# Recurrence preparation spread over the token-shift tiles, filter weights as sums and differences, expert slabs read among the last dense slabs

## Time and profile before

| | |
|---|---|
| median of three runs | 2147.86 us |
| the profiled execution | 2153.43 us |
| its span | 2151.6 us |
| mean granted TensorE clock | 0.923 |
| PE busy | 1889.2 us (88%) |
| DVE busy | 624.7 us (29%) |
| ACT busy | 295.8 us (14%) |
| POOL busy | 79.5 us (4%) |
| HBM read | 423.02 MB |
| expert slabs | 189 whole, 6 halves |

### The profile page before, as it was taken

The page is one execution under the profiler, slowest core; times in us unless marked ns, Lnnn a source line. Parts: engine busy times, 40 slices in busy tenths (PEclk is TensorE's granted clock), DMA queues, the critical chain, the costliest instruction groups (busy, mean ns, idle before and its releaser), DMA issues.

```text
span 2151.6 us, 26763 instructions
## 1 busy us (share of the span) xinstructions
PE 1889.2 (88%) x10986; PEld 1306.1 (61%) x10986; DVE 624.7 (29%) x1253; ACT 295.8 (14%) x664; POOL 79.5 (4%) x95
## 2 busy tenths in 40 slices
PE   7999999999999999999999997999997656565665
PEld 2444445888874787679889985887777212121212
DVE  4544445031432213624000348250434000000001
ACT  2200000011210012402000233211322000000001
POOL 1000000010000000001000102120001000000000
PEclk9999999999999999989999999797998788786868
DMA  8544444444432122136446731000238899999995
GB/s 325 181 165 170 173 175 163 145 151 157 149 126 71 51 95 98 59 134 220 153 156 240 250 137 59 3 3 20 79 118 329 361 421 421 422 422 422 422 422 242
DMA packets 64248, 425.45 MB, mean 198 GB/s; under 512 B 7283, under 2 KB 7764, under 8 KB 16988
## 3 DMA queue, kind: packets, MB, share of 16 engines
q1 hardware_dynamic: 54576, 387.05, 46.9%
q10 hardware_dynamic: 9580, 37.05, 4.9%
HBM read 423.02 MB, written 1.05 MB: 197 GB/s over the span
## 4 chain that ended last, share of the span: by engine, by line
PE 30%; DMA 19%; DVE 3%; SPq 1%; issue 1%; POOL 1%; ACT 1%; POOLq 0%; ACTq 0%; DVEq 0%
PE bank L785 19%; DMA arena<-experts_dram 19%; PE bank L1220 3%; PE bank L1470 2%; PE bank L1099 1%; SPq L708 1%; PE bank L1289 1%; DVE arena L2391 1%; PE bank L1306 1%; PE bank L1304 1%; PE bank L1292 0%; PE bank L1345 0%; PE bank L1392 0%; PE bank L1320 0%; POOL rstd L735 0%
## 5 line engine op out<-in xcount | busy, mean ns | idle before, releaser
L785 PE MATMUL bank<-arena 128*128 128x256 f32 (+2 forms) x4864 | 1117.6, 391 | 4.6 <-DVE arena L2266 2.0
L785 PEld LDWEIGHTS bank<-arena 128*128 128x128 f32 x4864 | 832.6, 192 | 280.0 <-issue 199.8
L1470 PE MATMUL bank<-arena 128*32 128x512 f32 x1536 | 251.4, 816 | 182.5 <-DMA arena<-experts_dram 182.5
L1470 PEld LDWEIGHTS bank<-arena 128*32 128x32 f32 x1536 | 66.5, 143 | 361.6 <-issue 361.6
L2091 DVE TENSOR_TENSOR arena<-sil,bank 128x512 f32 (+3 forms) x44 | 24.4, 554 | 275.9 <-PE bank L785 265.8
L2582 DVE TENSOR_TENSOR arena<-arena,bank 128x512 f32<-128x512 f32 x8 | 5.5, 689 | 275.4 <-PE bank L1470 275.4
L1604 ACT ACTIVATE sil<-bank 128x512 f32<-128x512 f32 (+1 forms) x44 | 21.6, 491 | 401.8 <-PE bank L785 239.8
L1220 PE MATMUL bank<-arena 64*64 64x64 f32 x2048 | 66.4, 227 | 7.8 <-POOL arena L754 5.5
L1220 PEld LDWEIGHTS bank<-arena 64*64 64x64 f32 x2048 | 65.4, 143 | 9.3 <-POOL arena L754 5.7
L2097 DVE SCALAR_TENSOR_TENSOR sq<-arena 128x1024 f32<-128x1024 f32 x56 | 68.4, 1222 | 1.5
L2098 DVE SCALAR_TENSOR_TENSOR arena<-arena 128x1024 f32<-128x1024 f32 x56 | 68.3, 1220 | 0.0
(11 more groups left out here) (331 smaller groups left out, 1418.3 us busy)
## 6 DMA issues: line engine op xcount, KB each, us to landing
arena<-experts_dram SPq DMA_DIRECT2D x189, 1024.0 KB, 22.9
arena<-dense_dram SPq DMA_DIRECT2D x167, 1024.0 KB, 4.8
arena<-ada_rest_dram ACTq DMA_DIRECT2D x56, 512.0 KB, 3.8
arena<-ada_head_dram SPq DMA_DIRECT2D x8, 1024.0 KB, 25.4
arena<-experts_dram SPq DMA_DIRECT2D x6, 512.0 KB, 22.8
arena<-tokens_dram ACTq DMA_DIRECT2D x1, 2048.0 KB, 22.5
arena<-masks_dram ACTq DMA_DIRECT2D x1, 1184.0 KB, 5.1
arena<-decay_dram ACTq DMA_DIRECT2D x1, 1024.0 KB, 15.8
```

The lines of the kernel that those rows point to most:

```text
L785: ins = mm(out, lhsT=w, rhs=rhs(k), start=k == 0, stop=k == k_tiles - 1)
L1470: ins = mm(ps[banks[half]][32 * e:32 * e + 32, :], lhsT=lhs[:, 2 * kp + par, CAP * e:CAP * e + CAP], rhs=slab[e][par][:, half * 512:half * ...
```

## The change

Four edits.

1. **Filter.** The third sine layer stands ahead of the first conditioning product. It is computed twice, on partitions 0 to 63 and 64 to 127 (`filt_w3` laid out twice), and of the second copy only column 0 is used, with its sign turned; the rest of those rows is zero. w4 comes as 128 rows, and POOL makes sum and difference of its halves once. Eight products by these give sum and difference at once, four of them over 128 rows; DVE has one multiplication for each. The second conditioning product is moved between the two halves.
2. **Preparation.** Its steps are placed between the shift tiles on each engine; `k_dir` goes to POOL; the low-rank products use banks 7, 5 and 6; ACT takes the gate's sigmoid after the aq tiles; `BT`, `KT` and `QQ` are made in the order in which they are wanted, with events of their own; AM is cleared in three parts.
3. **Expert slabs.** SP issues twelve ring slabs and one of the three extra ones between the dense slabs 151 to 163, then four and the two others. The extra three are now slabs 16 to 18.
4. **End.** The last four slabs come in halves, all first halves ahead of all second ones, and ACT loads the square root's table before the last group's copies.

```diff
             pe.wait_ge(filters_in, 32)
             sine_layer(0)
             sine_layer(1)
+            sine_layer(2)
             pe.wait_ge(cond_ready, 1)
             ada_sums("ada_head", 0, 0)
-            sine_layer(2)
...
+            pe.wait_ge(w4_ready, 2)
             pe.wait_ge(sin_ready, 3)
             for n in range(8):
+                half, tt, part = n // 4, n // 2 % 2, n % 2
+                rows = (P, 64)[tt]
+                take(pe, "w4", n % 4, half)
+                mm(ps[n % 4][:, :], lhsT=fh[0:rows, tt * P:tt * P + P], rhs=w4_parts[part][0:rows, half * 512:half * 512 + 512],
+                   start=True, stop=True).then_inc(full[n % 4], 1)
+                if n == 3:
+                    ada_sums("ada_head", 0, 1)
...
@@ gpsimd
+            pool.wait_ge(w4_in, 16)
+            for n, op in enumerate((add, sub)):
+                nc.gpsimd.tensor_tensor(w4_parts[n], w4[:, 0:D], w4[:, D:2 * D], op).then_inc(w4_ready, 1)
...
+            pool.wait_ge(mu_ready, 1)
+            for n in range(4, 8):
+                evacuated(pool, "lora", *lora_at(n))
+            for d in range(2):
+                for j in range(4):
+                    nc.gpsimd.tensor_scalar(kd256[:, 4 * d + j, :], iclr[:, 4 * d + j, :], c("ka", j), tiny[:, 28 + j:29 + j],
+                                            mult, add).then_inc(kd_scaled, 1)
+            pool.wait_ge(kkr_ready, 1)
+            for d in range(2):
+                pool.wait_ge(kd_scaled, 4 * d + 4)
+                nc.gpsimd.tensor_tensor(kd256[:, 4 * d:4 * d + 4, :], kd256[:, 4 * d:4 * d + 4, :], US[:, US_K:US_K + 4, :], mult)\
+                    .then_inc(kd_ready, 1)
+            pool.wait_ge(kt_ready, 1)
+            nc.gpsimd.memset(page(19, 2048), 0.0).then_inc(am_zero, 1)
+            pool.wait_ge(exc_used, 1)
+            nc.gpsimd.memset(page(21, 4096), 0.0).then_inc(am_zero, 1)
             pool.wait_ge(qq_ready, 1)
-            nc.gpsimd.memset(page(19, 8192), 0.0).then_inc(am_zero, 1)
+            nc.gpsimd.memset(page(20, 2048), 0.0).then_inc(am_zero, 1)
@@ tensor
             for t in range(len(EARLY), 15):
                 b, use = shift_at(t)
                 take(pe, "shift", b, use)
                 product(ps[b][:, 0:T], KD, lambda k: h[:, k, :], full[b])
+                if t == 7:
+                    pe.wait_ge(masks_in, 48)
+                    kk_norm()
+                elif 8 <= t < 12:
+                    if t == 8:
+                        pe.wait_ge(act_us, 1)
+                        evacuated(pe, "shift", 1, 0)
+                    for n in range(2 * t - 16, 2 * t - 14):
+                        lora_up(n)
@@ scalar
+            def decays(d):
+                act.wait_ge(logs_ready, d + 1)
+                ...
+                A(Eneg[:, o, :], inc[:, o, :], ACT.Exp, scale=DECAY_SCALE)
+                A(Eexc[:, o, :], (D2, D1)[d][:, o, :], ACT.Exp, scale=(-DECAY_SCALE, DECAY_SCALE)[d])
+                A(Einc[:, o, :], inc[:, o, :], ACT.Exp, scale=-DECAY_SCALE)
+                A(scl[:, 4 * d:4 * d + 4], scl[:, 4 * d:4 * d + 4], ACT.Exp, scale=-DECAY_SCALE).then_inc(exps_ready, 1)
             for t in range(15):
                 b, use = shift_at(t)
                 got(act, "shift", b, use)
                 A(US[:, t, :], ps[b][:, 0:T], ACT.Copy, scale=rt[:, 256 + t:257 + t]).then_inc(us_scaled, 1)
+                if t == 6:
+                    evacuated(act, "shift", 0, 0)
+                    A(US[:, 0, :], US[:, 0, :], ACT.Tanh).then_inc(act_us, 1)
+                    act.wait_ge(kkr_ready, 1)
+                    A(gsq_kk, kkr_flat, ACT.Square).then_inc(kksq_ready, 1)
+                elif t == 8:
+                    act.wait_ge(ss_ready, 1)
+                    A(nrm, nrm, ACT.Sqrt).then_inc(nrm_ready, 1)
+                if 8 <= t < 12:
+                    for n in range(2 * t - 16, 2 * t - 14):
+                        lora_out(n)
+                elif t >= 13:
+                    decays(t - 13)
@@ vector
+            for t in range(15):
+                shifted(t)
+                if t == 5:
+                    kk_scaled()
+                elif t == 7:
+                    kk_sums()
+                elif t == 9:
+                    dve.wait_ge(nrm_ready, 1)
+                    do(V.reciprocal(nrm, nrm))
+                elif t == 11:
+                    decay_sums(0)
+                elif t == 12:
+                    decay_logs(0)
+                elif t == 13:
+                    decay_sums(1)
+                elif t == 14:
+                    decay_logs(1)
@@ sync
+            mixer2 = N_DENSE - 31
+            for m in range(first_mixed * RING, N_DENSE):
                 sp.wait_ge(slab_started, m - RING + 2)
                 sp.dma_start(ring_flat[m % RING], dram["dense"][m]).then_inc(slab_loaded[m % RING], 16)
+                if m == mixer2 + 15:
+                    got(sp, "gn", 3, 0)
+                    expert(0, 1, 2)
+                elif m == mixer2 + 21:
+                    evacuated(sp, "batt", 7, 3)
+                    sp.wait_ge(yr_ready, 1)
+                    expert(3, 4, 5)
+                elif m == mixer2 + 22:
+                    expert(6, 7)
+                elif m == mixer2 + 23:
+                    expert(8)
+                    got(sp, "proja", 3, 1)
+                    expert(9)
+                elif m == mixer2 + 24:
+                    expert_late(0)
+                elif m == mixer2 + 26:
+                    evacuated(sp, "projr", 3, 1)
+                    expert(10)
+                elif m == mixer2 + 27:
+                    expert(11)
+            got(sp, "wout", 3, 3)
+            expert(12, 13, 14, 15)
+            expert_late(1)
+            for half in range(2):
+                got(sp, "htok", 5 + half, 1)
+            expert_late(2)
...
+            for par in range(2):
+                for e in range(GROUP):
+                    j = rest - GROUP + e
+                    sp.wait_ge(ex_started, rounds * EX_RING + (j + EX_LATE) // GROUP * GROUP + 2 * GROUP)
+                    sp.dma_start(ex_flat[j][:, par * D:par * D + D], dram["experts"][12 * N_EXP - GROUP + e][:, par * D:par * D + D])\
+                        .then_inc(ex_last_in[e] if par else ex_loaded[j], 16)
```

More of the change, by code:

```diff
@@ L1136, in _, with kk_norm, lora_up @@
             half_tiles("shift", 5, shift_norms)
+            def kk_norm():
+                pe.wait_ge(kksq_ready, 1)
+                for i in range(2):
+                    take(pe, "kkn", 5 + i, 0)
+                    mm(ps[5 + i][:, :], lhsT=blk, rhs=gsq_kk[:, i * 512:i * 512 + 512], start=True, stop=True)\
+                        .then_inc(full[5 + i], 1)
+            def lora_up(n):
+                which, d, half = n // 4, n // 2 % 2, n % 2
+                b, use = lora_at(n)
+                take(pe, "lora", b, use)
+                for q_ in range(2):
+                    j = 2 * half + q_
+                    ins = mm(ps[b][:, q_ * T:q_ * T + T],
+                             lhsT=lora[64 * d:64 * d + 64, which * 512 + j * P:which * 512 + j * P + P],
+                             rhs=US[64 * d:64 * d + 64, which, :], start=True, stop=True)
+                ins.then_inc(full[b], 1)
             for t in range(len(EARLY), 15):
```

326 lines of the change are left out of this document (151 added, 175 removed).

## The result

| | before | after |
|---|---|---|
| median | 2146.96 us (4 runs, 2143.56 to 2148.00) | 2117.79 us (4 runs, 2113.02 to 2119.78) |
| profiled execution | 2153.43 us | 2117.58 us |
| its span | 2151.6 us | 2115.7 us |
| mean granted TensorE clock | 0.923 | 0.930 |

The ratio after to before is 0.9864, 95% interval [0.9843, 0.9884]: 29.2 us less by the medians. The forecast was 2117 us, range 2105 to 2129. The total came out, in part by luck: of its four terms two were off in opposite directions and made up for most of each other.

What follows compares the result with a forecast made beforehand. Expert-stage transfers at 421 GB/s were taken as the bound, so time saved ahead of them is saved whole. Terms 0 + 8.5 + 17.9 + 4.6 = 31.0 us gave a 2117 us median, range 2105 to 2129.

Steps and rivals of the forecast that it cites:

- Start: Kernel start: earlier sine layer and possible early clock rise set against later w4 and GpSimd sums; 0 us taken.
- rival 4: Kernel start: the TensorE clock rises early, 5 us more gained, 2112 us; chance 0.05.
- Preparation: Recurrence preparation: steps placed between shift tiles bring the first masked copy 10 us earlier, less 1.5 for clock: 8.5 us.
- The gap: Before the first aq tile: TensorE stands 4.5 us because ScalarE's exponentials precede its copy of the last shift tile.
- The contention: Recurrence preparation: GpSimd's work slows VectorE's logs and scans beside it; 2 us taken, 8 at most.
- rival 1: Recurrence preparation: GpSimd holds VectorE up and the preparation gains nothing; total gain about 22 us, 2126; chance 0.14.
- its sign: Recurrence preparation: a first masked copy 8 to 10 us nearer to the shift's last tile would show the forecast.
- Rival 1's rule: Recurrence preparation: two-input elementwise work is about half as fast on GpSimd, which shares SBUF interfaces with VectorE.
- Expert start: First expert product: no 13.5 us transfer wait, 3.4 us from full clock, 1 from the ramp; 17.9 us.
- the ramp: Start of expert stage: four slots coming free at once speed the rate's rise; 1 us taken, 1.8 at most.
- Rivals 2 and 3: Expert start: slabs still land after the gather, 2133 us (0.08); or expert slabs starve the dense stream, 2157 at most (0.03).
- Tail: Kernel end: half slabs shorten the last product by 3.3 us and the table load moves ahead; together 4.6 us.

Runs made afterwards that it cites:

- 64-row run: Changed kernel with the w4 products of token tile 0 on 64 rows instead of 128: 2120.95 us, ratio 0.9891 to the kernel before.
- both orders: Changed kernel with ScalarE's direction-0 exponentials behind its last copy and VectorE's second scans behind its last shift: 2110.98 us, ratio 0.9830 to before.
- its own experiment: Changed kernel with the last four slabs whole and the table load where it was before: 2126.11 us, ratio 0.9907 to before.

## Why the prediction was right, and where not

The sum was 31.0 us, the medians gave 29.2. The edits by themselves say where it was lucky: the first two terms, 0 and 8.5 in the forecast, gave 4.8 and 1.2, so two errors of 5 and 7 us left 2.5 in the sum. By its steps:

- **Start, taken as 0 with bounds of 3 either way; measured 6.1 in the profile and 4.8 by the filter edit alone.** This step failed, and rival 4 (chance 0.05) is what happened. The two prices were in hand, 0.85 and 0.43 us a record; the prediction worked out up to 5 us from them and gave none to the term. The profiles, that of the 64-row run above all, show that the 128-row products do it. Of the parts beside it, w4 landed 10.1 us after its issue and not 14, which gave room for GpSimd's sums; the contention of these sums with the sine layer was not in the working at all and took it back.
- **Preparation, taken as 8.5; measured 5.3 at the first masked copy and 1.2 at the end by the edit alone.** The 3.2 us missing at the copy are in three steps. TensorE's loop from the first full tile to the end of the last took 41.5 us, not 39.7: the four pairs of low-rank products took 7.7 and not 6.9, the tiles 32.0 and not 31.1. The gap was foreseen at 4.5 us and 5.60 came, but the step named ScalarE's exponentials for it and VectorE ended it; here the mechanism was wrong. From the gap's end to the copy it took 29.3 us, not 28.9, in which the clock cost 1.8 where 1.5 was taken: the aq tiles took 19.34 us, with both orders 17.53. The contention was taken as 2 us; logarithms, small product, large product and scans lost 0.34 + 0.16 + 2.24 + 1.26 = 4.0. In no step was the half-clock spell 50 us further on, whose long form takes 5 us back. By itself the preparation thus did what rival 1 said, nothing, but only in part by rival 1's mechanism: without GpSimd's work the gap is 2.7 us shorter and the copy 1.5 us earlier.
- **Two slips in that step.** With contention and clock in full (8 and 3.5 us, where 2 of contention are in the 10 already) its working leaves 10 - 6 - 3.5 = 0.5 us and not 2. And its sign, a copy 8 to 10 us nearer to the shift's last tile, fits its working only if it is read from the first full tile, where 5.3 was measured; from the end of the last tile it was 50.5 us before and 34.9 after.
- **Rival 1's rule.** GpSimd took 5.64 us for two 128x1024 products of which VectorE does two in 2.36, 2.4 times; the first took 2.35 us, 2.0 times, and the second ran beside VectorE's scans. The Trainium skill (GPSIMD Engine Reference, 4.1 Engine selection) says about twice for two inputs, and the trace agrees; it has one-input work near line rate there, and here the scalings took 2.2 times VectorE's time (6.01 against 2.68), and still 1.6 times in the six of them that followed each other at 0.54 us. The measurement decides.
- **Expert start, taken as 17.9; measured 16.9**, 14.3 + 3.1 less the 0.5 of the stage behind. The wait went as worked out (13.5 us; the other 0.8 of the 14.3 is the gather, 5.6 us instead of 6.3), and the product at full clock gave 3.1 where 3.4 was taken. The 1 us for the ramp did not: the rate rose in two steps and not in four, but the stage was no shorter. Rivals 2 and 3 did not occur; TensorE waited for no slab between 1574 and 1660 us.
- **Tail, taken as 4.6; measured 4.0 in the profile, 5.0 by its own experiment.** The last product fell by 3.4 us (3.3 taken); over all profiles it took 5.1 to 6.5 us with whole slabs and 1.9 to 3.3 with halves. Of the table load's 1.28 us about 0.8 was hidden before: ScalarE now waits 0.79 us for TensorE at that place.

## What to carry to other kernels

When work is spread between other work, list for each in-order engine what stands ahead of the instruction that frees the critical one: of two engines in a row only the later shows in the profile, and changing the other gains nothing until it is changed too. Work moved to GpSimd is not free cover: price the VectorE operations that run beside it, and ask whether VectorE could do it a little later in half the time. Read a gain again behind the next spell at half clock before booking it, and read it from more than one profile: here the same instruction took 3.46 us in one and 1.21 in the next.

## What the runs showed of the hardware

- At the start TensorE ran at two speeds (8 conditioning records in 1.93 or 1.07 us) while the granted clock reads 1.00 throughout, up to 39.9 us in the kernel with 64 rows. Two lines of the table of stretches, the kernel with 64 rows at its 1.93 us:

```profile
26.00:30.00 4.00, 4.00 (x12) 1.11 (x12) 0.69 (x1) 1.78 (x3) 3.12 (x3) 1.00 1.04 425
```

and the kernel after at its 1.07 us:

```profile
22.00:26.00 4.00, 4.00 (x15) 0.99 (x14) 2.20 (x4) 1.15 (x2) 0.03 (x1) 1.00 0.98 408
```

  That it is the half clock is inferred from the factor; the column does not show it there, since the trace's clock records begin only when TensorE gets fast.
- Products on 64 rows left TensorE at the slow speed for all 16 records, in each of five profiles. With 128 rows in half of them it rose within the first eight in eight profiles and within the second eight in one.
- Beside GpSimd's two-input work a 128x1024 product took VectorE 3.46 us instead of 1.22 and eight scans 3.88 instead of 2.62, or 1.21 and 5.99, with GpSimd's own product at 3.40 us instead of 2.35. A one-input 128x256 operation took 2.31 us, and 0.29 without it.
- In the recurrence TensorE fell to half clock in every profile, 49 to 59 us behind the first masked copy: 1.5 to 1.9 us after a wait of 1.6 us and for 20.5 to 23.9 us, or 8.0 to 9.8 us after the same wait, out of unbroken work, and for 10.2 us. One program, the kernel before, showed both.
